# Four direct pairs instead of six in each FFN of an encoder layer, with the row factors, the first granule and the down projection's waits rearranged

## The chip, the cores and the metric

The kernel runs on one core of a Trainium2 chip. The metric is the device time of one execution in microseconds. A core has the matrix engine TensorE (PE), VectorE (DVE), ScalarE (ACT), GpSimd (POOL) and SyncE (SP), which here only issues DMAs. Each engine works through its own instructions in order, and semaphores are all that ties one to another.

## The reference, cut to what matters

One encoder layer on x of 512 rows and 1024 columns in float32:

```python
x = x + 0.5 * swiglu(rms(x, g_ffn1), w_up1, w_down1)      # FFN 1, r = 0
x = x + mixer(rms(x, g_mix))                              # attention, Fourier mix, gates
x = x + 0.5 * swiglu(rms(x, g_ffn2), w_up2, w_down2)      # FFN 2, r = 1
out = rms(x, g_final)

def swiglu(h, w_up, w_down):                              # D_FF = 2816
    gate, up = split(h @ w_up)
    return (silu(gate) * up) @ w_down
```

`rms` divides each row by the root of its mean square (plus 1e-6) and multiplies by a gain. The change touches only the two FFNs and the way x comes in.

## The kernel before, in words

Everything is held transposed: features on the 128 partitions, the 512 rows of x along the free axis. x is 8 tiles of 128 x 512, the activations of an FFN are 22 tiles (`a_t`). Each float32 factor is split into a high part, rounded to the format that TensorE multiplies at its faster rate (`_hi`, by ScalarE, line 575), and the remainder (`_lo`, by VectorE: line 953 for weights, 957 for other tensors, 1121 for the weights of window pairs). A product is then three passes: high by high, high by low, low by high.

A *granule* is 128 columns of a weight matrix with all its input tiles: for the up projection 8 tiles, so 24 matmuls of 512 columns (`granule`; lines 1484 and 1485 are the passes with the high weights, 1496 the pass with the low ones, 1489 that pass where it goes tile by tile). Its weights go through four slots: `raw` (DMA on SP), `w_hi`, `w_lo`. A slot is loaded again when `w_lo_ready` says that the remainder four granules earlier is made, and split again when `w_used` says that TensorE is done with it. A *pair* is one tile of gate and the tile of up that belongs to it.

Each FFN has two ways for a pair. The first six pairs are *direct*: two granules, whose banks VectorE multiplies by the row factors `rstd` (`gate`, `up`); then ScalarE takes silu and VectorE multiplies (`swish`). The row factors are thus not needed when the product starts, only when its bank is read. They come from the squares (ScalarE), added up by GpSimd (line 1430), summed over the partitions by tiny matmuls (`sum_squares`, line 1520), then mean (VectorE, 990), power (GpSimd, 1434), diagonal (VectorE, 978) and a broadcast by a matmul with ones (`spread_factors`, 1527). The other sixteen pairs are *window pairs*: a pair's 1024 x 256 weights and h are cut into 2 x 2 blocks and multiplied by a scheme with seven products of blocks instead of eight (`pair_frame`, lines 1593, 1595, 1599). It needs h with its row factors applied (`normed_h`, 1095), four differences of h blocks (`T_1` to `T_4`, on GpSimd, 1443), the high part and remainder of seven such blocks (`t_rounded`, `t_rest`), and for each pair four sums of weight blocks: two on VectorE (`sums`, 1111 and 1112), two on GpSimd (s2 and s4, 1450 and 1452). A frame's weights are four groups, G0 to G3. In a frame TensorE runs G0 x T_B11, G0 x T_2, the last product of the pair before, G1 x T_B21, G1 x T_4, G2 x T_1 and G2 x T_3; before the last of these it waits for `u2`, a sum that VectorE forms (1128).

All this preparation is interleaved by hand into the direct pairs. There is no planner: the order on each engine is the order of the lines in `direct_pairs` (one function for ScalarE, one for VectorE) and, for GpSimd, the four differences and then two sums per pair. TensorE runs the direct granules (`ffn_up`), the frames, and `ffn_down`. In the down projection a block of 128 output columns is four granules that split the 22 activation tiles by `DOWN_TILES`; the first block waits for the rounding of the activations (`a_rounded`, `a_rest`, in the order `CONV`, two tiles a step), once for each granule.

At the start x comes in four DMA pieces of two tiles, and the weights of granules 0 to 3 behind or between them. TensorE transposes the tiles (`x_tile`, 1536). `X_ORDER` is the order in which ScalarE and VectorE take the transposed tiles: "h" makes the high part and remainder of the unscaled h, "x" copies the tile, "s" squares it, "w" splits a weight granule.

## Time and profile before

| | us |
|---|---|
| median of 3 runs (1012.06 to 1014.20) | 1013.02 |
| the profiled execution | 1014.11 |
| its span, first to last instruction | 1012.3 |

| engine | busy us | share of the span |
|---|---|---|
| PE, matmuls | 997.7 | 99% |
| DVE | 679.0 | 67% |
| ACT | 440.1 | 43% |
| POOL | 198.1 | 20% |

Busy time of PE counts every microsecond in which a matmul is under way; matmuls overlap, so their durations (0.39 us for one of 512 columns) are longer than the distance between their starts (0.23 us). The profiled execution's mean granted TensorE clock is 0.995 of 2.4 GHz. In this profile the first FFN's direct granules run from 12.4 to 83.3 us, its frames to 243.3, the down projection behind it; the second FFN's first up granule starts at about 650 and its first frame at 717.

### The profile page before, as it was taken

The numbers are of one execution on the slowest core, as the hardware profiler recorded it, in microseconds if no ns is written. First come the engines' busy times: TensorE is split into PE (matmuls) and PEld (weight loads), VectorE is DVE, ScalarE is ACT, GpSimd is POOL, SyncE is SP. The second block draws the span as 40 slices with busy tenths as digits, with TensorE's granted clock in tenths as the row PEclk, the third lists the DMA queues.
The fourth block names the chain that finished last, engine by engine and source line by source line (L and its number), as shares of the span: only waits on it lengthen the run. The fifth ranks groups of instructions, "written<-read, shape, count | busy, mean of one in ns | idle before, by whom it ended". The sixth has DMA issues, their size and how long they took to land. (4 is left out here: it accounts for less than half of the span.)

```text
span 1012.3 us, 16276 instructions
## 1 busy us (share of the span) xinstructions
PE 997.7 (99%) x5872; PEld 885.7 (87%) x5872; DVE 679.0 (67%) x924; ACT 440.1 (43%) x656; POOL 198.1 (20%) x113
## 2 busy tenths in 40 slices
PE   8999999999999999999999999999999999999997
PEld 7789999999788888888888888888999999978887
DVE  5778999999534346667765555458899999943332
ACT  5344444446322325346664334334445454633322
POOL 2452333340011110000000001324234333001101
PEclk9999999999999999999999999999999999999999
DMA  6423334323433364212213343322333332333222
GB/s 210 132 66 94 116 92 120 87 83 96 124 96 90 115 171 125 63 42 62 63 42 89 98 124 104 104 84 72 96 108 100 110 97 83 89 117 96 88 68 84
DMA packets 191816, 98.81 MB, mean 98 GB/s; under 512 B 13384, under 2 KB 190616, under 8 KB 191648
## 3 DMA queue, kind: packets, MB, share of 16 engines
q1 hardware_dynamic: 190560, 95.50, 32.3%
q10 hardware_dynamic: 1216, 2.78, 0.8%
q8 instruction: 25, 0.41, 0.2%
q14 instruction: 15, 0.12, 0.0%
HBM read 96.15 MB, written 2.11 MB: 97 GB/s over the span
## 5 line engine op out<-in xcount | busy, mean ns | idle before, releaser
L575 ACT ACTIVATE w_hi<-raw 128x1024 fp32r<-128x1024 f32 (+2 forms) x202 | 181.5, 902 | 231.6 <-PE bank L1496 155.2
L953 DVE TENSOR_TENSOR w_lo<-raw,w_hi 128x1024 fp32r<-128x1024 f32 (+2 forms) x138 | 150.0, 1089 | 145.7 <-ACT w_hi L575 144.2
L1595 PE MATMUL bank<-t_lo,w_hi 128*128 128x256 f32 x896 | 224.7, 283 | 0.0
L1593 PE MATMUL bank<-t_hi,w_hi 128*128 128x256 f32 x896 | 224.6, 283 | 0.0
L1595 PEld LDWEIGHTS bank<-t_lo,w_hi 128*128 128x128 f32 x896 | 172.0, 192 | 0.2
L1593 PEld LDWEIGHTS bank<-t_hi,w_hi 128*128 128x128 f32 x896 | 172.0, 192 | 0.2
L1430 POOL TENSOR_TENSOR ssum<-ssum,sq 128x512 f32<-128x512 f32 x27 | 41.4, 1533 | 535.2 <-ACT sq L612 534.4
L1599 PE MATMUL bank<-t_hi,w_lo 128*128 128x256 f32 x896 | 144.0, 283 | 0.0
L1484 PE MATMUL bank<-a_hi,w_hi 128*128 128x512 f32 (+1 forms) x374 | 140.6, 380 | 1.7 <-ACT a_hi L575 1.7
L1485 PE MATMUL bank<-a_lo,w_hi 128*128 128x512 f32 (+1 forms) x374 | 139.4, 377 | 0.0
L1599 PEld LDWEIGHTS bank<-t_hi,w_lo 128*128 128x128 f32 x896 | 123.6, 192 | 0.0
L1121 DVE TENSOR_TENSOR w_lo<-raw,w_hi 128x1024 fp32r<-128x1024 f32 x64 | 90.9, 1420 | 9.3 <-ACT w_hi L575 9.3
L575 ACT ACTIVATE w_hi<-raw_b 128x1024 fp32r<-128x1024 f32 x64 | 60.8, 949 | 80.0 <-POOL raw_b L1450 40.4
L1121 DVE TENSOR_TENSOR w_lo<-raw_b,w_hi 128x1024 fp32r<-128x1024 f32 x64 | 92.8, 1449 | 3.8 <-ACT w_hi L575 3.7
L1496 PE MATMUL bank<-a_hi,w_lo 128*128 128x512 f32 (+1 forms) x374 | 91.1, 377 | 0.0
L1484 PEld LDWEIGHTS bank<-a_hi,w_hi 128*128 128x128 f32 x374 | 70.3, 188 | 15.4 <-ACT a_hi L575 2.5
L1484 PE MATMUL bank<-h_hi,w_hi 128*128 128x512 f32 x208 | 81.9, 394 | 0.3 <-DVE ga_t L1270 0.3
L1485 PEld LDWEIGHTS bank<-a_lo,w_hi 128*128 128x128 f32 x374 | 70.4, 188 | 12.6
L1485 PE MATMUL bank<-h_lo,w_hi 128*128 128x512 f32 x208 | 81.1, 390 | 0.0
L1496 PEld LDWEIGHTS bank<-a_hi,w_lo 128*128 128x128 f32 x374 | 67.8, 188 | 12.9
L1484 PE MATMUL bank<-hf_hi,w_hi 128*128 128x512 f32 x192 | 76.2, 397 | 0.0
L1485 PE MATMUL bank<-hf_lo,w_hi 128*128 128x512 f32 x192 | 75.7, 394 | 0.0
(230 smaller groups left out, 1494.6 us busy)
## 6 DMA issues: line engine op xcount, KB each, us to landing
raw<-in_w_down_dram SPq DMA_DIRECT2D x48, 384.0 KB, 3.0
raw_b<-in_w_up_dram SPq DMA_DIRECT2D x64, 256.0 KB, 3.7
raw<-in_w_up_dram SPq DMA_DIRECT2D x64, 256.0 KB, 3.6
raw<-in_w_up_dram SPq DMA_DIRECT2D x24, 512.0 KB, 3.9
raw<-in_w_in_dram SPq DMA_DIRECT2D x22, 512.0 KB, 3.7
raw<-in_w_down_dram SPq DMA_DIRECT2D x32, 128.0 KB, 2.2
raw<-in_w_out_dram SPq DMA_DIRECT2D x8, 512.0 KB, 3.4
x_rows<-in_x_dram SPq DMA_DIRECT2D x4, 512.0 KB, 7.8
```

What stands on the lines that cost most here:

```text
L575: return nc.scalar.activation(dst, src, ACT.Copy, scale=scale)
L953: vec.tensor_tensor(w_lo[:, s, 0:nk, :], raw[:, s, 0:nk, :], w_hi[:, s, 0:nk, :].bitcast(F32), ALU.subtract).then_inc(w_lo_ready, 1)
L1121: vec.tensor_tensor(w_lo[:, slot, 0:nk, :], pair_raw[q % 2][:, slot, 0:nk, :], w_hi[:, slot, 0:nk, :].bitcast(F32), ALU.subtract).then_inc ...
L1430: nc.gpsimd.tensor_tensor(ssum[:, :], ssum[:, :], sq[:, m % 2, :], ALU.add).then_inc(sum_added, 1)
L1484: nc.tensor.matmul(out_ap, w_hi[:, s, k, :], xh, start=first and i == 0, stop=False)
L1485: mm = nc.tensor.matmul(out_ap, w_hi[:, s, k, :], xl, start=False, stop=False)
L1496: mm = nc.tensor.matmul(out_ap, w_lo[:, s, k, :], x_parts(k)[0], start=False, stop=last and i == len(tiles) - 1)
L1593: nc.tensor.matmul(out_ap, w_hi[:, slot, at_ + k, :], hi[:, k, :], start=first and k == 0, stop=False, skip_group_check=not first)
L1595: nc.tensor.matmul(out_ap, w_hi[:, slot, at_ + k, :], lo_[:, k, :], start=False, stop=False, skip_group_check=not first)
L1599: mm = nc.tensor.matmul(out_ap, w_lo[:, slot, at_ + k, :], hi[:, k, :], start=False, stop=k == HK - 1, skip_group_check=not first)
```

## The change

Of 22 pairs in each FFN, four are direct and eighteen are window pairs. The row factors' squares are summed inside granule 2 and broadcast ahead of granule 3 in the first FFN, and summed behind granule 0 and broadcast inside granule 1 in the second. Only two tiles of x are transposed ahead of granule 0; four more stand before its tile 2 and the last two before its tile 4, and `X_ORDER` changes with it. In the first block of the down projection TensorE waits for every second tile instead of once for each granule, the tiles of the last granule are taken in the order 0, 1, 20, 21, and ScalarE and VectorE take three more conversions ahead of the last split. The steps of `direct_pairs` are put in a new order on both engines.

```diff
@@ -38,12 +38,12 @@
 SLOTS = 4
 BANKS = 4
 
-DOWN_TILES = [list(range(14, 20)), list(range(2, 8)), list(range(8, 14)), [20, 21, 0, 1]]
+DOWN_TILES = [list(range(14, 20)), list(range(2, 8)), list(range(8, 14)), [0, 1, 20, 21]]
 DOWN_PARTS = [len(tiles) for tiles in DOWN_TILES]
 assert sorted(sum(DOWN_TILES, [])) == list(range(FK)) and len(DOWN_PARTS) == SLOTS
 
 
-DIRECT = 6
+DIRECT = 4
 PAIRS = FK - DIRECT
 assert DIRECT % 2 == 0 and PAIRS % 2 == 0
 UP_GRANULES = 2 * DIRECT + SLOTS * PAIRS
@@ -106,10 +106,9 @@
 
 
 X_BANKS = 6
-X_ORDER = [("h", 0), ("w", 0), ("h", 1), ("h", 2), ("x", 0), ("h", 3), ("h", 4), ("x", 1), ("h", 5),
-           ("h", 6), ("s", 0), ("h", 7), ("x", 2), ("w", 1), ("x", 3), ("x", 4), ("s", 1), ("s", 2),
-           ("s", 3), ("x", 5), ("x", 6), ("x", 7), ("w", 2), ("s", 4), ("s", 5), ("s", 6), ("s", 7),
-           ("w", 3)]
+X_ORDER = [("h", 0), ("w", 0), ("h", 1), ("x", 0), ("x", 1), ("h", 2), ("s", 0), ("h", 3), ("s", 1), ("x", 2),
+           ("h", 4), ("h", 5), ("s", 2), ("x", 3), ("h", 6), ("h", 7), ("x", 4), ("x", 5), ("x", 6), ("x", 7),
+           ("w", 1), ("s", 3), ("s", 4), ("s", 5), ("s", 6), ("s", 7), ("w", 2), ("w", 3)]
 NREL = 2 * WINDOW + 1
 ROWS = 4 * DK + 2 * DK
 
@@ -478,12 +477,14 @@
             def down(r, m, j, n=0):
                 g = G_DOWN[r] + j
                 cols = slice(m * P, (m + 1) * P) if isinstance(m, int) else bass.ds(sp.snap(m * P), P)
-                k0, nk = DOWN_TILES[j][0], DOWN_PARTS[j] if j < SLOTS - 1 else 2
-                load(g, raw[:, g % SLOTS, 0:nk, :], w_down[r][:, k0:k0 + nk, cols], m, n)
-                if j == SLOTS - 1:
-                    k1 = DOWN_TILES[j][2]
+                if j < SLOTS - 1:
+                    k0, nk = DOWN_TILES[j][0], DOWN_PARTS[j]
+                    load(g, raw[:, g % SLOTS, 0:nk, :], w_down[r][:, k0:k0 + nk, cols], m, n)
+                else:
+                    k0, k1 = DOWN_TILES[j][0], DOWN_TILES[j][2]
+                    load(g, raw[:, g % SLOTS, 2:4, :], w_down[r][:, k1:k1 + 2, cols], m, n)
                     cols = slice(m * P, (m + 1) * P) if isinstance(m, int) else bass.ds(sp.snap(m * P), P)
-                    sp.dma_start(raw[:, g % SLOTS, nk:2 * nk, :], w_down[r][:, k1:k1 + nk, cols]).then_inc(down_second, 16)
+                    sp.dma_start(raw[:, g % SLOTS, 0:2, :], w_down[r][:, k0:k0 + 2, cols]).then_inc(down_second, 16)
 
 
             xv = x[0].rearrange("(t p) d -> p t d", p=P)
@@ -651,28 +652,22 @@
                     direct_hi(r, j)
                 silu(r, 0)
                 silu(r, 1)
+                t_rounded(r, T_B11)
                 direct_hi(r, 7)
+                t_rounded(r, T_1)
+                t_rounded(r, T_B21)
+                t_rounded(r, T_2)
                 if r == 0:
                     act.wait_ge(row_ready, 1)
                     act.dma_start(bias_rows, bias_row[:, :]).then_inc(bias_stored, 16)
-                t_rounded(r, T_B11)
-                direct_hi(r, 8)
-                t_rounded(r, T_1)
-                t_rounded(r, T_B21)
-                direct_hi(r, 9)
-                t_rounded(r, T_2)
+                t_rounded(r, T_4)
                 silu(r, 2)
-                t_rounded(r, T_4)
-                direct_hi(r, 10)
                 t_rounded(r, T_3)
                 t_rounded(r, T_B22)
-                silu(r, 3)
-                direct_hi(r, 11)
                 group_hi(r, 0, G0)
-                silu(r, 4)
                 group_hi(r, 0, G1)
                 group_hi(r, 0, G2)
-                silu(r, 5)
+                silu(r, 3)
 
             def t_rounded(r, t):
 
@@ -763,13 +758,12 @@
                 for i in (4, 5, 6):
                     a_rounded(r, CONV[i])
                 split_hi(g + 2)
-                a_rounded(r, CONV[7])
+                for i in (7, 8, 9):
+                    a_rounded(r, CONV[i])
                 silu_c12(r, q)
-                a_rounded(r, CONV[8])
                 act.wait_ge(w_used, g + 1)
                 split_hi(g + 3)
-                for i in (9, 10):
-                    a_rounded(r, CONV[i])
+                a_rounded(r, CONV[10])
 
             def turned_rows(m, odd):
 
@@ -1042,51 +1036,44 @@
                 nrm = NORM_FFN1 if r == 0 else NORM_FFN2
                 direct_lo(r, 4)
                 mean(nrm)
-                direct_lo(r, 5)
                 diagonal(nrm)
-                direct_lo(r, 6)
+                if r == 0:
+                    direct_lo(r, 5)
                 factors(nrm)
                 gate(r, 0)
                 up(r, 0)
+                for i in range(HK):
+                    normed_h(nrm, i)
+                if r == 1:
+                    direct_lo(r, 5)
                 gate(r, 1)
+                swish(r, 0)
+                for i in range(HK, DK):
+                    normed_h(nrm, i)
+                direct_lo(r, 6)
                 up(r, 1)
-                swish(r, 0)
                 if r == 0:
                     constants()
-                for i in range(HK):
-                    normed_h(nrm, i)
                 swish(r, 1)
+                t_rest(r, T_B11)
                 direct_lo(r, 7)
-                for i in range(HK, DK):
-                    normed_h(nrm, i)
-                direct_lo(r, 8)
+                t_rest(r, T_2)
                 gate(r, 2)
+                t_rest(r, T_B21)
+                sums(r, 0)
                 up(r, 2)
+                t_rest(r, T_4)
                 swish(r, 2)
-                t_rest(r, T_B11)
-                t_rest(r, T_2)
-                direct_lo(r, 9)
+                t_rest(r, T_1)
+                group_lo(r, 0, G0)
                 gate(r, 3)
-                t_rest(r, T_B21)
-                up(r, 3)
-                direct_lo(r, 10)
-                swish(r, 3)
-                t_rest(r, T_4)
-                t_rest(r, T_1)
-                direct_lo(r, 11)
-                sums(r, 0)
-                gate(r, 4)
                 t_rest(r, T_3)
-                group_lo(r, 0, G0)
-                up(r, 4)
-                swish(r, 4)
+                group_lo(r, 0, G1)
                 t_rest(r, T_B22)
-                group_lo(r, 0, G1)
-                gate(r, 5)
                 group_lo(r, 0, G2)
                 sums(r, 1)
-                up(r, 5)
-                swish(r, 5)
+                up(r, 3)
+                swish(r, 3)
 
             def normed_h(n, m):
 
@@ -1192,12 +1179,12 @@
                 for i in (4, 5, 6):
                     a_rest(r, i)
                 split_lo(g + 2)
+                a_rest(r, 7)
+                a_rest(r, 8)
                 c12(r, q)
-                a_rest(r, 7)
+                a_rest(r, 9)
                 swiglu(r, q)
-                a_rest(r, 8)
                 split_lo(g + 3)
-                a_rest(r, 9)
                 a_rest(r, 10)
 
             def residual(n, m, o, scale, it=0, per=0):
@@ -1467,8 +1454,7 @@
                 return mm
 
             def granule(g, out_ap, x_parts, first=True, last=True, it=0, n=0, tiles=None, x_ready_at=None, done=True,
-                        by_tile=False,
-                        between=None):
+                        by_tile=False, between=None, inside=None):
 
 
 
@@ -1478,6 +1464,8 @@
                 for i, k in enumerate(tiles):
                     if between and by_tile:
                         between(k)
+                    if inside and k == DK // 2:
+                        inside()
                     if x_ready_at:
                         x_ready_at(k)
                     xh, xl = x_parts(k)
@@ -1547,7 +1535,7 @@
             pe.wait_ge(ident_ready, 2)
             pe.wait_ge(gain_landed, 16)
             nc.tensor.transpose(banks[0][:, 0:DK], gain_rows[:, :], ident[0:DK, 0:DK]).then_inc(gain_turned, 1)
-            for m in range(X_BANKS):
+            for m in range(2):
                 x_tile(m)
 
             def other_constants():
@@ -1561,8 +1549,8 @@
 
             def x_rest(k):
 
-                if k in (2, 4):
-                    x_tile(X_BANKS + k // 2 - 1)
+                for m in {2: range(2, 6), 4: range(6, DK)}.get(k, ()):
+                    x_tile(m)
 
             def ffn_up(r, it, first=False, n=SLOTS):
                 nrm = NORM_FFN1 if r == 0 else NORM_FFN2
@@ -1572,14 +1560,17 @@
                         pe.wait_ge(out_read, o - 3 + n * it)
                     if first and r == 0 and j >= 2:
                         pe.wait_ge(x_ready, DK)
+                    if first and r == 0 and j == 3:
+                        spread_factors(nrm)
                     granule(g, banks[o % BANKS][:, :], hf_parts, it=it, n=n, by_tile=first and j == 0,
                             x_ready_at=h_ready(nrm) if first and j == 0 else None,
                             between=x_rest if first and r == j == 0 else
-                            (lambda: spread_factors(nrm)) if first and j == 3 else None)
-                    if first and j == 2:
+                            (lambda: spread_factors(nrm)) if first and r == 1 and j == 1 else None,
+                            inside=(lambda: sum_squares(nrm)) if first and r == 0 and j == 2 else None)
+                    if first and r == 1 and j == 0:
                         sum_squares(nrm)
-                        if r == 0:
-                            other_constants()
+                    if first and r == 0 and j == 2:
+                        other_constants()
 
             def product(r, q, it, group, at_, t, out_ap, first=True):
 
@@ -1651,14 +1642,18 @@
                     for j in range(SLOTS):
                         g = G_DOWN[r] + SLOTS * c + j
 
-                        if first and c == 0:
-                            if j == 1:
-                                last_product(r, PAIRS - 1)
-                            need = len(CONV) * r + 1 + max(CONV.index(i // 2) for i in DOWN_TILES[j])
-                            pe.wait_ge(a_hi_ready, need)
-                            pe.wait_ge(a_lo_ready, need)
+                        if first and c == 0 and j == 1:
+                            last_product(r, PAIRS - 1)
+
+                        def a_ready(k, tiles=DOWN_TILES[j]):
+
+                            if k % 2 == 0:
+                                need = len(CONV) * r + 1 + CONV.index(tiles[k] // 2)
+                                pe.wait_ge(a_hi_ready, need)
+                                pe.wait_ge(a_lo_ready, need)
+
                         granule(g, banks[o % BANKS][:, :], a_parts(DOWN_TILES[j]), first=j == 0, last=j == SLOTS - 1,
-                                it=it, n=n)
+                                it=it, n=n, x_ready_at=a_ready if first and c == 0 else None)
                         if r == 1 and j == 1 and not (first and c == 0):
                             turn_rows(2 * it + c - 1, 1 - c)
```

## Rows read from the trace of the kernel before

**Rows 1.** The page, part 1: busy time, share of the span, instructions

```profile
PE 997.7 (99%) x5872; PEld 885.7 (87%) x5872; DVE 679.0 (67%) x924; ACT 440.1 (43%) x656; POOL 198.1 (20%) x113
```

**Rows 2.** Waits of TensorE, longest first: us in total, times, longest

```profile
PE bank L1536 <- DMA x_rows<-in_x_dram: 3.2, 1, 3.2
...
PE bank L1484 <- ACT a_hi L575: 1.7, 2, 0.9
```

**Rows 3.** TensorE's timeline, start to 75 us: start, duration, engine, line, operation

```profile
9.29 3.35 PE L1536 MATMUL bank<-ident,x_rows 128*128 128x128 f32 x16 [3.19 <-DMA x_rows<-in_x_dram]
...
30.16 1.05 PE L1520 MATMUL bank<-ones,ssum 128*128 128x2 f32 x8 [0.25 <-POOL ssum L1430]
...
31.86 0.50 PE L1484 MATMUL bank<-hf_hi,w_hi 128*128 128x512 f32 x1
...
37.22 1.02 PE L1527 MATMUL bank<-gb_t,ones 128*128 128x512 f32 x2
...
39.92 0.41 PE L1484 MATMUL bank<-hf_hi,w_hi 128*128 128x512 f32 x1
...
65.37 1.98 PE L1496 MATMUL bank<-hf_hi,w_lo 128*128 128x512 f32 x8
...
70.81 1.98 PE L1496 MATMUL bank<-hf_hi,w_lo 128*128 128x512 f32 x8
```

**Rows 4.** The same view in the pair frames

```profile
88.77 0.64 PE L1599 MATMUL bank<-t_hi,w_lo 128*128 128x256 f32 x4
...
90.21 0.64 PE L1599 MATMUL bank<-t_hi,w_lo 128*128 128x256 f32 x4
```

**Rows 5.** Busy time in one stretch, with TensorE's granted clock

```profile
33.00:34.00 1.00, 1.00 (x4) 0.72 (x3) 0.53 (x1) 0.00 (x0) 1.00 (x1) 0.50 1.03 304
```

**Rows 6.** VectorE's timeline before the first pair frame

```profile
38.28 0.69 DVE L984 COPY rstd<-bank 128x512 f32<-128x512 f32 x1 [1.82 <-PE bank L1527]
...
46.83 2.72 DVE L1095 SCALAR_TENSOR_TENSOR t_sum<-xT,consts,rstd 128x512 f32<-128x512 f32 x4
...
49.48 1.20 DVE L953 TENSOR_TENSOR w_lo<-raw,w_hi 128x1024 fp32r<-128x1024 f32 x1
...
58.51 4.56 DVE L957 TENSOR_TENSOR t_lo<-t_sum,t_hi 128x1024 fp32r<-128x1024 f32 x2
...
71.60 0.68 DVE L1111 TENSOR_TENSOR raw_b<-raw_b 128x512 f32<-128x512 f32 x1
...
72.81 0.68 DVE L1015 TENSOR_TENSOR ga_t<-bank,rstd 128x512 f32<-128x512 f32 x1
...
73.41 1.71 DVE L957 TENSOR_TENSOR t_lo<-t_sum,t_hi 128x1024 fp32r<-128x1024 f32 x1
...
75.17 2.19 DVE L1121 TENSOR_TENSOR w_lo<-raw_b,w_hi 128x1024 fp32r<-128x1024 f32 x1
...
86.64 0.42 DVE L1128 TENSOR_TENSOR u_t<-bank,p_t 128x256 f32<-128x256 f32 x1 [1.04 <-PE bank L1599]
```

**Rows 7.** GpSimd's differences and additions by line: least, median, longest ns

```profile
L1443 POOL TENSOR_TENSOR t_sum<-t_sum x8: 2401/2866/7701, 45.2 to 690.7; 128x1024 f32<-128x1024 f32 x8
...
L1430 POOL TENSOR_TENSOR ssum<-ssum,sq x27: 1289/1457/2092, 18.6 to 989.6; 128x512 f32<-128x512 f32 x27
```

**Rows 8.** Timelines at 28 and at 656 us, three engines

```profile
27.86 3.88 ACT L575 ACTIVATE w_hi<-raw 128x1024 fp32r<-128x1024 f32 x4
...
656.63 1.23 DVE L953 TENSOR_TENSOR w_lo<-raw,w_hi 128x1024 fp32r<-128x1024 f32 x1 [2.93 <-ACT w_hi L575]
...
658.91 1.98 PE L1496 MATMUL bank<-hf_hi,w_lo 128*128 128x512 f32 x8
...
667.15 0.16 DVE L990 TENSOR_SCALAR var<-bank 128x4 f32<-128x4 f32 x1 [9.29 <-PE bank L1520]
...
667.50 1.28 ACT L646 ACT_TABLE_LOAD   x1
...
669.35 0.87 DVE L978 TENSOR_SCALAR gb_t<-ident,rinv 128x128 f32<-128x128 f32 x4 [0.91 <-POOL rinv L1434]
```

## The prediction, made before the changed kernel was run

> **What bounds the kernel now.** I read the page's busy times first: TensorE is busy 99% of the span, so only its own instructions and its rare waits can set the time [rows 1]. The list of waits shows how rare they are: 3.2 us for x's arrival, and 1.7 us in two equal waits for ScalarE's rounding of the activations, one at the head of each down projection [rows 2]. Then TensorE's timeline, for the price of what is exchanged. A direct granule repeats every 5.44 us (65.37 and 70.81), so a direct pair costs 10.88; a product of the seven-product scheme repeats every 1.44 us (88.77 and 90.21), so a pair costs 7 x 1.44 = 10.08 [rows 3, 4]. Last I read VectorE's and GpSimd's timelines between the row factors and the first pair frame, because the change takes 21.8 us of TensorE time away from that stretch. There the reader is to see that VectorE hardly rests, and that its operations on two SBUF tensors and GpSimd's shut each other out [rows 6, 7].
>
> Sums are made against the profiled execution: 1014.11 us for a span of 1012.3. The median of the runs shown is 1013.02, 1.09 below; I apply the difference to the median. About 0.2% (2.0 us) is what a measurement can tell from nothing.
>
> **Four pairs moved from direct to seven products.** 4 x (10.88 - 10.08) = -3.2 us, certain as TensorE work at full clock.
>
> **Down projection waits by tile.** The third granule of the first column block waited for all six tiles though the first four were ready. With waits by tile, and with tiles 10 to 13 rounded before the last pair's swish, the two waits go: -1.7 us [rows 2]. What is late next is tiles 20, 21; they need VectorE's last product, split and remainder, but [0, 1, 20, 21] puts them 0.9 us into a granule that starts after the removed wait. I estimate they arrive level with it. Ends: -1.7 and, if the last product is late by as much, 0.
>
> **The start.** Tiles 0 and 1 of granule 0 now run before x's second piece lands at 9.29, in time in which TensorE waited [rows 2, 3]. But VectorE's low halves come at 9.3, so tile 1 runs behind the landing, and ScalarE and VectorE now alternate squares and copies with the h tiles; I follow both and get granule 0 done within 0.2 us of before. Then a new wait: the third granule's split stands behind the eighth square on ScalarE, and that square waits for GpSimd's fifth addition. The additions need at least 1.29 us each, 1.46 in the median [rows 7], the third can't start before about 18.8 (behind the split of granule 1), so the square ends at 24.4 and the split, 0.97 us apiece [rows 8], at 25.4; granule 1 ends at 24.2. TensorE waits 1.2 us. Against it, the factors are now taken earlier: squares summed inside granule 2 (1.0), constants (0.7) and then the broadcast. It needs split, sum, power and diagonal on VectorE and GpSimd: VectorE reaches the mean at about 29.9 behind three w_lo, and from the mean's start to the diagonal's end is 3.07 us (667.15 to 670.22) [rows 8]. So the broadcast starts at about 33.0, 0.4 after TensorE is free. It keeps TensorE 0.9 (37.22 to 39.92 is 2.70 with 1.81 of low products behind it) [rows 3], granule 3 takes 5.44, and granule 4 starts at 39.3 instead of 39.92: -0.6 us. This includes 1.7 us gained because the clock need not fall: at 33 to 34 us the granted clock was 0.50, which is 1.2 of 2.4 GHz, after a wait and 1.7 us of tiny matmuls (30.16 to 31.86), and from 31.86 to 39.92 stand 8.06 us for 0.89 + 5.44 = 6.33 of work: 1.7 lost [rows 3, 5]. If it falls here too, the term is +1.1; if it also stays full at 9 us, -1.6.
>
> **Row factors in the second FFN.** Sums behind granule 0, broadcast inside granule 1. Granule 1's high products end at 658.91 + 0.95 = 659.86. VectorE takes the mean only behind w_lo of granule 4, which ends at 657.86; plus 3.07, the diagonal is there at 660.95. TensorE had 0.5 us to spare here and now waits +1.1 us, with the low products queued behind it [rows 8]. Ends: 0.9 and 1.3.
>
> **The first pair frame of the first FFN.** This decides. Count from the broadcast's start E. Before, the frame began at E + 46.2 (37.22 to 83.4: 2.70 and eight granules). Now it begins at E + 0.89 + 5 x 5.44 = E + 28.1. Its last product needs VectorE's u2, 7.2 us later: E + 35.3. Before, that need was E + 53.4, and VectorE began u2 at 86.64 = E + 49.4 [rows 6]. VectorE's work from the factors' copy (E + 1.06) to u2, free of interference, by pitch: 0.60 for a 512-wide product (71.60 to 72.81 for two), 0.66 for a scaled h (46.83 to 49.48 for four), 1.14 for a remainder of 1024 (1.20 with the end overlapping) [rows 6]. Now it is: factors' copy, gate 0 and up 0, 1.9; eight scaled h, 5.3; the other two gates and up 1 to 3 with the third gate, 3.6 for six; four swish, 2.4; w_lo 6 and 7, 2.3; seven t remainders, 8.0; two pairs of sums, 2.4; three group remainders, 3.4; constants 0.5. Together 29.8: ready at E + 30.9, 4.4 us before the need.
>
> But GpSimd must place four 1024-wide differences and three 512-wide ones in it. How they interfere is in the rows: the remainder at 73.41 took 1.71 instead of 1.20, the one at 75.17 took 2.19, two at 58.51 took 4.56 instead of 2.35; each time it is GpSimd's rest, and one t difference took 7.7 us where the median is 2.87 and the least 2.40 [rows 6, 7]. So I take them as exclusive: 2.4 us for a wide difference, 1.2 for a narrow one (72.81 to 73.98). That is 4 x 2.4 + 3 x 1.2 = 13.2 us, less what falls beside VectorE's operations that read a bank (gates, ups, constants: at most 4.1). Before, 5.7 us of idle VectorE took two of them for nothing; that idle time is gone. Bounds: u2 at E + 30.9 (no exclusion: no loss) and E + 30.9 + 13.2 = E + 44.1 (+8.8). Placed in program order, I get: four scaled h until 5.6; T_1's difference beside gate 1 and into swish 0, until 8.2; scaled h 4 to 7 and w_lo 6 until 12.5; T_2 beside up 1 until 15.0; swish 1, T_4, B11, w_lo 7 and T_3 in either order, and T_2's remainder at E + 23.8 whichever side gets the turns, since all of it excludes itself; then gate 2, B21, sums, up 2 until 27.4, the narrow difference s2 until 28.0, and s4 among T_4, swish 2, T_1 and G0. So G0's remainder ends at E + 32.0 to 33.2 (needed at E + 29.1), and after gate 3, T_3, G1, B22, G2, sums, up 3, the next s2 and swish 3, u2 at E + 41.2 to 41.8: +6.0 us, about 3 to 4 of it at G0 and the rest before T_3. Waiting behind w_lo and u2 on TensorE is the whole frame, and behind that all that follows. Frames 1 to 17 then run as before, VectorE having slack in each.
>
> The Trainium skill ("SBUF — State Buffer", section "Who interferes with whom") says that a VectorE instruction with two SBUF inputs and a GpSimd instruction that reads SBUF block each other fully, and one with a single SBUF input does not. The trace agrees: 2.19 at 75.17 against 0.68 for a gate. By the rule the term is the 6.0 above; were it only a slowdown in proportion, it would be half.
>
> **The same frame in the second FFN.** Here the broadcast is two granules earlier, so the need is at E + 42.5. But gate 1 waits for granule 2, and silu 0 stands behind the split of granule 6 and a table load of 1.28 us, which was hidden at 667.50 [rows 8]. So swish 0 comes at E + 11.2, the chain runs 3.0 us behind that of the first FFN, and u2 comes at E + 44.2 to 44.8: +2.0 us (ends: 0 and 3).
>
> **Clock after the new waits.** Two waits of 2 to 4 us within 10 us; a fall costs the 1.7 above where TensorE is the bound, but between the two waits it isn't. I take +0.8 (0 to 3.4). "TensorE: Matmul & The Clock Gate" in the Trainium skill (section "HAM oscillation — how this bites in real kernels") warns that waits between bursts of matmuls bring the clock down each time; the half clock at 33 us after sparse work agrees, and by it this term would be 1.7 to 3.4.
>
> No other queue is in the way: SP issues the window loads after seven or eight w_lo as before and they land before the sums need them; POOL's order is unchanged; only the bias row's store moves on ScalarE's queue.
>
> **Sum.** -3.2 - 1.7 - 0.6 + 1.1 + 6.0 + 2.0 + 0.8 = +4.4: 1013.0 + 4.4 = 1017.4 us.
>
> **Rivals.**
> A. The preparation stays hidden: GpSimd's work falls in bank-reading operations and costs VectorE nothing, so terms of 6.0, 2.0 and 0.8 go: 1013.0 - 4.4 = 1008.6, faster. For it: before, VectorE was ahead by 4.0 us at u2 and idle for 6.7. Against it: 4.4 us of slack must hold 9.1 or more of exclusive work. It decides from the point where the blocked time is under 4.4.
> B. Half late: the first frame waits 4.0, the second FFN's doesn't, the clock stays: -4.4 + 4.0 = -0.4, 1012.6. For it: 9.1 - 4.4 = 4.7 is the least the budget allows, and the last narrow difference can fall behind u2 (-1.2).
> C. As forecast, and the clock falls at each wait and at the start: 1017.4 + 1.7 + 1.7 = 1020.8.
>
> Chances: forecast 0.52 (own range 1014.8 to 1019.5), A 0.16, B 0.20, C 0.12. The range 1010.5 to 1020.5 leaves out most of A and the upper half of C. Slower by over 0.2%: forecast and C, 0.64; within: B without its lower edge, 0.19; faster 0.17.
>
> **What the profile after would show.** TensorE waiting for VectorE's w_lo or u2 at about 61 to 75 us, 6 us in all, and VectorE without idle time from 34 on; t differences with GpSimd durations far over 2.4; a wait of 1.2 us for the split before the third granule; 1.1 us for the diagonal in the second FFN; no wait at the activations' rounding; granted clock 1.00 near 33 us; first activation product of the down projection at about 247 to 248 instead of 243.3. I am wrong if TensorE runs through the first frame: then VectorE's remainders aren't held up as I have placed them, and the time is A's.

## The result, and the profile after

The changed kernel takes 1016.15 us (median of 7 executions, 1015.56 to 1017.14) where the kernel before takes 1013.02 (median of 7): the ratio is 1.0035, with a 95% interval of 1.0024 to 1.0045. It is slower by 3.1 us. The profiled execution took 1016.41 us for a span of 1014.6, which is 2.3 above that of before. Lines below are those of the changed kernel.

Part 1 of the page, against [rows 1]:

```profile
PE 998.2 (98%) x6016; PEld 891.4 (88%) x6016; DVE 704.8 (69%) x948; ACT 448.1 (44%) x672; POOL 207.8 (20%) x121
```

TensorE's list of waits, against [rows 2]:

```profile
PE bank L1590 <- DVE w_lo L1108: 2.7, 1, 2.7
PE bank L1584 <- DVE u_t L1115: 2.0, 2, 1.5
...
PE bank L1472 <- ACT w_hi L576: 1.9, 2, 1.1
```

Busy time is 0.5 us more and not 3.2 less: time at half clock and short waits count as busy in it, so it is not where a change of this size is read. The two waits for a_hi are gone; in their place stand waits for VectorE's w_lo and u2, and for ScalarE's split. Where they fall is in TensorE's timeline of the first FFN (start, duration, engine, line, operation, idle time before it and its releaser):

```profile
11.23 3.59 PE L1524 MATMUL bank<-ident,x_rows 128*128 128x128 f32 x16
...
26.27 0.47 PE L1472 MATMUL bank<-hf_hi,w_hi 128*128 128x512 f32 x1 [0.79 <-ACT w_hi L576]
...
33.57 1.13 PE L1515 MATMUL bank<-gb_t,ones 128*128 128x512 f32 x2
...
62.09 0.39 PE L1584 MATMUL bank<-t_hi,w_hi 128*128 128x256 f32 x1 [0.16 <-ACT w_hi L576]
...
66.06 1.22 PE L1590 MATMUL bank<-t_hi,w_lo 128*128 128x256 f32 x4 [2.75 <-DVE w_lo L1108]
...
74.44 0.39 PE L1584 MATMUL bank<-t_hi,w_hi 128*128 128x256 f32 x1 [0.47 <-DVE u_t L1115]
...
75.98 0.28 PE L1584 MATMUL bank<-t_hi,w_hi 128*128 128x256 f32 x1
```

x's transposes start 1.9 us later than before (11.23 against 9.29 in [rows 3]); the third granule waits 0.79 for its split; the broadcast is at 33.57, so E = 33.57. The first frame starts at 62.09, stops for 2.75 us after its first eight matmuls and again at its last product, and the next frame follows at 75.98. In the kernel before the same two frames began like this:

```profile
83.50 0.28 PE L1593 MATMUL bank<-t_hi,w_hi 128*128 128x256 f32 x1
...
92.13 0.28 PE L1593 MATMUL bank<-t_hi,w_hi 128*128 128x256 f32 x1
```

(The prediction read 83.4 for the first.)

VectorE's timeline of the same stretch, against [rows 6]:

```profile
34.73 0.69 DVE L978 COPY rstd<-bank 128x512 f32<-128x512 f32 x1 [0.84 <-PE bank L1515]
...
39.91 2.53 DVE L1022 TENSOR_TENSOR a_t<-ga_t,ua_t 128x512 f32<-128x512 f32 x1
...
48.95 3.42 DVE L951 TENSOR_TENSOR t_lo<-t_sum,t_hi 128x1024 fp32r<-128x1024 f32 x1
...
52.30 3.41 DVE L947 TENSOR_TENSOR w_lo<-raw,w_hi 128x1024 fp32r<-128x1024 f32 x1
...
64.79 1.21 DVE L1108 TENSOR_TENSOR w_lo<-raw_b,w_hi 128x1024 fp32r<-128x1024 f32 x1
...
73.98 0.41 DVE L1115 TENSOR_TENSOR u_t<-bank,p_t 128x256 f32<-128x256 f32 x1
```

Behind 34.73 no row has an idle time before it until 74.6. A swish product at 39.91 took 2.53 us instead of 0.68, a remainder at 48.95 took 3.42 instead of 1.20. GpSimd's timeline shows what ran beside them: the first t difference at 39.48, and the other three in one piece, 3.15 us each. The last fence has the eight of the two FFNs by line, against [rows 7]:

```profile
39.48 2.42 POOL L1430 TENSOR_TENSOR t_sum<-t_sum 128x1024 f32<-128x1024 f32 x1 [7.62 <-DVE t_sum L1082]
45.17 9.46 POOL L1430 TENSOR_TENSOR t_sum<-t_sum 128x1024 f32<-128x1024 f32 x3 [3.28 <-DVE t_sum L1082]
```

```profile
L1430 POOL TENSOR_TENSOR t_sum<-t_sum x8: 2416/3314/3377, 39.5 to 684.1; 128x1024 f32<-128x1024 f32 x8
```

A table of the stages, each number but the span the start of an instruction in the two timelines of TensorE:

| us | before | after | moved by |
|---|---|---|---|
| granule 4, first FFN | 39.92 | 40.02 | +0.1 |
| first frame | 83.50 | 62.09 | -21.4 (21.76 of direct work less) |
| second frame | 92.13 | 75.98 | -16.2 |
| first down projection | 243.33 | 247.71 | +4.4 |
| attention block, first h_hi matmul | 365.9 | 368.9 | +3.0 |
| second FFN | 649.84 | 652.81 | +3.0 |
| second down projection | 876.83 | 880.51 | +3.7 |
| span | 1012.3 | 1014.6 | +2.3 |

Each FFN's up part loses time (4.4 and 0.7 us) and each down projection gives back 1.4.

### The profile page after: what moved, and what is told of

The parts are those of the page before. It is cut to its first block, busy times and chain, and to the rows that moved or that the text cites. A ratio compares the mean times of both kernels' runs of the same rounds, so it can differ in the third digit from the quotient of the medians.

```text
span 1014.6 us, 16714 instructions
## 1 busy us (share of the span) xinstructions
PE 998.2 (98%) x6016; PEld 891.4 (88%) x6016; DVE 704.8 (69%) x948; ACT 448.1 (44%) x672; POOL 207.8 (20%) x121
## 4 chain that ended last, share of the span: by engine, by line
PE 89%; DVE 5%; ACT 2%; issue 2%; POOL 1%; DMA 1%; POOLq 0%; ACTq 0%; SPq 0%; DVEq 0%
PE bank L1472 17%; PE bank L1473 17%; PE bank L1484 16%; PE bank L1584 11%; PE bank L1590 11%; PE bank L1586 11%; DVE w_lo L1108 1%; ACT w_hi L576 1%; DVE t_lo L951 1%; PE bank L1477 1%; PE bank L1756 1%; PE bank L1449 1%; PE bank L1448 1%; PE bank L1453 1%; DMA raw<-in_w_up_dram 1%
## 5 line engine op out<-in xcount | busy, mean ns | idle before, releaser
L1584 PE MATMUL bank<-t_hi,w_hi 128*128 128x256 f32 x1008 | 253.9, 284 | 2.4 <-DVE u_t L1115 2.0
L1586 PE MATMUL bank<-t_lo,w_hi 128*128 128x256 f32 x1008 | 253.4, 284 | 0.0
L1584 PEld LDWEIGHTS bank<-t_hi,w_hi 128*128 128x128 f32 x1008 | 194.0, 192 | 3.7 <-DVE u_t L1115 2.4
L1586 PEld LDWEIGHTS bank<-t_lo,w_hi 128*128 128x128 f32 x1008 | 194.0, 192 | 0.1
L1590 PE MATMUL bank<-t_hi,w_lo 128*128 128x256 f32 x1008 | 162.8, 284 | 2.7 <-DVE w_lo L1108 2.7
L1590 PEld LDWEIGHTS bank<-t_hi,w_lo 128*128 128x128 f32 x1008 | 139.8, 193 | 3.0 <-DVE w_lo L1108 3.0
L1108 DVE TENSOR_TENSOR w_lo<-raw,w_hi 128x1024 fp32r<-128x1024 f32 x72 | 103.4, 1437 | 6.2 <-ACT w_hi L576 6.2
L1108 DVE TENSOR_TENSOR w_lo<-raw_b,w_hi 128x1024 fp32r<-128x1024 f32 x72 | 102.5, 1424 | 3.7 <-ACT w_hi L576 3.7
L1472 PE MATMUL bank<-hf_hi,w_hi 128*128 128x512 f32 x128 | 51.7, 404 | 1.9 <-ACT w_hi L576 1.9
L1437 POOL TENSOR_TENSOR raw<-raw 128x512 f32<-128x512 f32 x18 | 30.1, 1672 | 114.0 <-DVE raw L1098 114.0
```

What stands on the lines that cost most here:

```text
L1108: vec.tensor_tensor(w_lo[:, slot, 0:nk, :], pair_raw[q % 2][:, slot, 0:nk, :], w_hi[:, slot, 0:nk, :].bitcast(F32), ALU.subtract).then_inc ...
L1437: nc.gpsimd.tensor_tensor(s2, a22, s3, ALU.subtract).then_inc(s2_ready, 1)
L1472: nc.tensor.matmul(out_ap, w_hi[:, s, k, :], xh, start=first and i == 0, stop=False)
L1584: nc.tensor.matmul(out_ap, w_hi[:, slot, at_ + k, :], hi[:, k, :], start=first and k == 0, stop=False, skip_group_check=not first)
L1586: nc.tensor.matmul(out_ap, w_hi[:, slot, at_ + k, :], lo_[:, k, :], start=False, stop=False, skip_group_check=not first)
L1590: mm = nc.tensor.matmul(out_ap, w_lo[:, slot, at_ + k, :], hi[:, k, :], start=False, stop=k == HK - 1, skip_group_check=not first)
```

## Experiments

Each was timed beside the kernel before on the same chip; its ratio is to that. The theory: VectorE and GpSimd exclude each other in the preparation, which makes u2 of the first pair late, and all else is small.

**1, 2. The tile waits alone**, in the kernel before (t1_tiles), with the rounding order of the last pair that belongs to them. The same kernel was run again as e11_tiles; it is called kernel 1 below.

```
-DOWN_TILES = [..., [20, 21, 0, 1]]
+DOWN_TILES = [..., [0, 1, 20, 21]]
...
-                            pe.wait_ge(a_hi_ready, need)
+                        def a_ready(k, tiles=DOWN_TILES[j]):
+                            if k % 2 == 0:
+                                need = len(CONV) * r + 1 + CONV.index(tiles[k] // 2)
...
```

> The kernel before with one part of the change alone: waits by tile in the first block of the down projection, its tiles in the order 0, 1, 20, 21, and the conversions ahead of the last split. If the term is what the two removed waits were (0.86 and 0.88 us), it is 1.7 us faster than before: 1011.3. If what the two traces show between the first and the last granule of that block holds (1.4 us in each FFN), 2.8 us faster: 1010.2. If the last product of VectorE takes the wait's place: 1013.

> The kernel before with waits by tile once more, beside e9 on the same chip, to compare the two: 1009.7 us as in its first runs. The theory has it ahead of e9 by 1.5 to 3 us, since six direct pairs hide what four don't.

1009.73 us, ratio 0.9972 (0.9962 to 0.9982), and 1010.73, ratio 0.9981 (0.9972 to 0.9989): -3.4 and -2.0 us. From the first activation product to the first of the attention block it takes 121.1 us (241.5 to 362.6) where the kernel before takes 122.6. Worth 1.4 us in each FFN, not 0.85. Why more than the wait: before, 13.74 us pass from the first product to the third granule's low pass (243.33 to 257.07), after it 12.4 (247.7 to 260.1); 0.86 of the difference is the wait in brackets; the other 0.5 has no bracket.

**3. The t differences at half width.** Half of each difference is left out of the computation, filled with zeros; VectorE's work stays whole.

```
+                        nc.gpsimd.memset(t_sum[:, to, HK // 2:HK, :], 0.0)
-                        nc.gpsimd.tensor_tensor(t_sum[:, to, :, :], ...
+                        nc.gpsimd.tensor_tensor(t_sum[:, to, 0:HK // 2, :], ...
```

> The changed kernel with GpSimd's four t differences only half as wide (the other half is filled with zeros, so half of each difference is left out of the computation). VectorE's work and all waits are unchanged. Theory (GpSimd's and VectorE's operations on two SBUF tensors exclude each other, and that makes VectorE late): each difference holds the port 1.2 us less, VectorE reaches the last u2 some 4 us earlier, TensorE's waits for VectorE in the first frames (2.7, 0.5 and 1.5 us) all but go, and with them the half clock: 1010 to 1012 us. Rival (VectorE's own work is too much for four direct pairs, whatever GpSimd does): the waits stay, 1015 to 1016.

1009.53 us, ratio 0.9966 (0.9956 to 0.9976): 6.6 us faster than the change. TensorE's waits, and u2 on VectorE's timeline:

```profile
PE bank L1473 <- ACT w_hi L576: 1.7, 2, 1.0
...
PE bank L1585 <- DVE u_t L1115: 1.2, 1, 1.2
```

```profile
69.62 0.41 DVE L1115 TENSOR_TENSOR u_t<-bank,p_t 128x256 f32<-128x256 f32 x1
```

The wait for w_lo is gone, u2 comes 4.4 us earlier, with VectorE's own instructions unchanged. Only GpSimd's time was taken away, so it was GpSimd's time that made VectorE late.

**4. The change with the old start of the first FFN** (x's order, squares and broadcast as before):

```
-X_ORDER = [("h", 0), ("w", 0), ("h", 1), ("x", 0), ("x", 1), ("h", 2), ("s", 0), ...
+X_ORDER = [("h", 0), ("w", 0), ("h", 1), ("h", 2), ("x", 0), ("h", 3), ("h", 4), ...
-                    if first and r == 0 and j == 3:
-                        spread_factors(nrm)
```

> The changed kernel with the start of the kernel before in the first FFN: six tiles of x transposed first, the old X_ORDER, squares summed behind granule 2 and the broadcast inside granule 3. Granule 4 then starts at about 39.9 us as in both kernels, but the broadcast at about 37.2 instead of 33.6. Theory (the first frame is set by VectorE, whose chain starts with the broadcast): all behind the first frame comes 3.6 us later, 1019 to 1020 us, and TensorE's waits in the first frame grow by as much. Rival (TensorE sets the time and the earlier broadcast is worth only what it saves of TensorE's own time): 1016 to 1016.5.

1018.08 us, ratio 1.0051 (1.0036 to 1.0067), 1.9 us slower than the change, between the two expectations. In its timeline of TensorE:

```profile
36.49 1.02 PE L1516 MATMUL bank<-gb_t,ones 128*128 128x512 f32 x2
...
39.19 0.39 PE L1473 MATMUL bank<-hf_hi,w_hi 128*128 128x512 f32 x1
...
64.85 0.38 PE L1583 MATMUL bank<-t_hi,w_hi 128*128 128x256 f32 x1 [3.72 <-ACT w_hi L577]
...
78.74 0.28 PE L1583 MATMUL bank<-t_hi,w_hi 128*128 128x256 f32 x1
```

Granule 4 begins at 39.19, 0.8 earlier than in the change; the second frame begins at 78.74, 2.76 later, and E is 2.92 later. So the new start is worth nothing on TensorE. It is worth E, because VectorE's chain counts from there. Part of the 2.92 is the clock and not the order: in this execution it fell at the start, as it did before the change:

```profile
33.00:34.00 1.00, 1.00 (x4) 0.82 (x3) 1.00 (x5) 0.00 (x0) 0.00 (x0) 0.50 1.15 347
```

Where it stayed up, in the two executions of kernel 1 (experiment 9), the same start has E at 35.39 and 34.73 instead of 36.49.

**5. The power beside a remainder.** In the changed kernel the diagonal went ahead of w_lo 5; this puts it back.

```
                 mean(nrm)
-                diagonal(nrm)
                 if r == 0:
                     direct_lo(r, 5)
+                diagonal(nrm)
```

> The changed kernel with VectorE's split of granule 5 moved between the mean and the diagonal in the first FFN, where the kernel before had it. Theory (VectorE's split and GpSimd's power exclude each other): the power takes 1.9 us instead of 1.02, the diagonal and the broadcast come 0.9 us later, and since the first frame is set from there, 1017.0 us. Rival (the power takes 1.02 because of something else): the split ends before the power does, nothing moves, 1016.2 us.

1016.19 us, ratio 1.0035 (1.0023 to 1.0047): no difference that the runs can tell. GpSimd's power and TensorE's broadcast in the timeline:

```profile
30.14 1.94 POOL L1421 TENSOR_TENSOR rinv<-var,half 128x4 f32<-128x4 f32 x1 [3.50 <-DVE var L984]
...
33.13 1.10 PE L1515 MATMUL bank<-gb_t,ones 128*128 128x512 f32 x2 [0.18 <-DVE gb_t L972]
```

and in the changed kernel the same power in the two FFNs:

```profile
30.83 1.02 POOL L1421 TENSOR_TENSOR rinv<-var,half 128x4 f32<-128x4 f32 x1 [3.50 <-DVE var L984]
...
660.98 1.02 POOL L1421 TENSOR_TENSOR rinv<-var,half 128x4 f32<-128x4 f32 x1 [3.17 <-DVE var L984]
```

Beside a remainder the power takes 1.94, without it 1.02. In the first FFN that moves next to nothing: TensorE waits 0.18 us for the diagonal here, and in the change it gets to the broadcast after the diagonal anyhow (33.57, the diagonal ends at 32.76).

**6, 7, 8. VectorE's order by need.** e6_order puts G0, T_3 and u2 ahead of work that is needed later; e7_w2 also splits granule 2's weights ahead of the last two squares; e9_tail mends what e6_order made late, with c2 of the first pair ahead of G3 and up 3 last, and on ScalarE G1's high part ahead of a silu.

```
# e6_order
                 t_rest(r, T_4)
+                group_lo(r, 0, G0)
                 swish(r, 2)
+                gate(r, 3)
+                group_lo(r, 0, G1)
                 t_rest(r, T_1)
-                group_lo(r, 0, G0)
...
+                t_rest(r, T_3)
+                u2(r, 0)
+                t_rest(r, T_B22)
+                group_lo(r, 1, G0)
                 up(r, 3)
# e7_w2, besides
-           ("w", 1), ("s", 3), ("s", 4), ("s", 5), ("s", 6), ("s", 7), ("w", 2), ("w", 3)]
+           ("w", 1), ("s", 3), ("s", 4), ("s", 5), ("w", 2), ("s", 6), ("s", 7), ("w", 3)]
# e9_tail, in the products of the first pair, over e6_order
+                if not q:
+                    c2(r, 0)
+                    group_lo(r, 0, G3)
+                    group_lo(r, 1, G1)
+                    up(r, 3)
+                    swish(r, 3)
```

> The changed kernel with VectorE's steps ahead of the first frame in the order in which TensorE needs them: G0's remainder ahead of swish 2 and T_1, G1's ahead of T_1, u2 and G0 of the next pair ahead of up 3 and swish 3. Nothing is added or taken away. Theory (the waits come from VectorE's order and from too little time, some 2 us too little in the first FFN, none in the second): TensorE's 2.7 us wait at G0 falls under 1, frame 1 of the first FFN starts at about 73 us instead of 76.0, the second FFN's 1.5 us wait goes: 1011.6 us. Rival (the sum of VectorE's work decides, and an order only moves the wait to another product): 1015 to 1016 us.

> The reordered kernel with ScalarE's and VectorE's split of granule 2 ahead of the last two squares at the start, instead of behind them. Theory (the third granule waits only for that split, 0.8 us in the changed kernel, and the broadcast is set by TensorE's own work from there): everything behind comes 0.8 us earlier, 1010.8 us. Rival (the last squares come 1 us later and the sum of squares, inside granule 2, takes over the wait): no difference to the reordered kernel, 1011.6 us.

> The reordered kernel (e6), which traded TensorE's wait at G0 for one of 3.0 us at the last product of pair 0 (behind c2(0) on VectorE, which stood behind up 3, swish 3 and G1's split, that on ScalarE behind a silu that waits for swish 3). Now c2(0) stands ahead of G3, up 3 and swish 3 behind G1 of the next pair, and G1's high part ahead of that silu. Same work. Theory (four direct pairs leave VectorE some 2 us too little in the first FFN and enough in the second, if each step stands where its product needs it): waits of 2 to 3 us in the first FFN, under 1 in the second, 1011 to 1013 us. Rival (the order moves the wait once more): 1015 us or more.

All three are misses, and slower: 1019.76 (ratio 1.0075, 1.0062 to 1.0089), 1024.29 (1.0122, 1.0106 to 1.0137), 1020.71 (1.0077, 1.0064 to 1.0090). TensorE's waits of e6_order and the row behind the longest of them:

```profile
PE bank L1586 <- DVE ua_t L1126: 5.9, 2, 3.0
PE bank L1592 <- DVE w_lo L1110: 2.4, 3, 1.0
```

```profile
80.42 0.39 PE L1586 MATMUL bank<-t_hi,w_hi 128*128 128x256 f32 x1 [2.96 <-DVE ua_t L1126]
```

and TensorE's longest wait of e9_tail:

```profile
PE bank L1590 <- ACT p_t L576: 4.4, 2, 2.2
```

In e6_order the second frame did begin at 72.7, as I had worked out. But what had been put back was needed 8 us on: 2.96 us for ua_t at 80.4, the same in the second FFN, and the down projection at 250.5 instead of 247.7. VectorE has no slack from 34.7 to 74.6, so each of the three orders only chose who waits, and chose worse; that no order would do better is not shown. In e7_w2 another wait took the place of the split's: 1.7 us for GpSimd's last sum. Its trace is of the fastest of its four executions (1020.98); why the others took up to 4 us more is open.

**9. The squares inside granule 3**, in kernel 1, to see whether earlier factors pay there.

```
+                            inside=(lambda: sum_squares(nrm)) if first and r == 0 and j == 3 else None)
```

> The kernel before with waits by tile (six direct pairs), and in the first FFN the squares summed inside granule 3 instead of behind granule 2, the split of granule 5 behind the diagonal. The tiny matmuls no longer stand in one piece with the wait and the constants. Theory (they brought the clock down to half at 32.6 us, 1.7 us lost): granted clock 1.00 at 33 us, 1.7 us off the 1009.7 of the kernel with waits by tile: 1008.0 us. Rival (the clock falls anyway, or the first gate is late for granule 4 and takes the time back): 1009 to 1010 us.

1010.49 us, ratio 0.9981 (0.9972 to 0.9990): level with kernel 1. TensorE waits 0.71 us for ga_t at 38.85. In kernel 1 there was nothing to get in the two executions that have a profile. The clock rows of 33 to 34 us (last three columns: granted clock, DMA share, GB/s), first of t1_tiles, then of e11_tiles:

```profile
33.00:34.00 1.00, 1.00 (x6) 0.82 (x5) 0.29 (x1) 0.00 (x0) 1.00 (x1) 1.00 1.12 328
```

```profile
33.00:34.00 1.00, 1.00 (x6) 0.84 (x5) 0.44 (x3) 0.00 (x0) 0.53 (x1) 1.00 0.96 281
```

Both are 1.00 where [rows 5] and the execution of experiment 4 have 0.50, with the same instructions on TensorE.

**10. The change without its tile waits.**

```
+                        if first and c == 0:
...
+                            need = len(CONV) * r + 1 + max(CONV.index(i // 2) for i in DOWN_TILES[j])
+                            pe.wait_ge(a_hi_ready, need)
```

> The changed kernel without its tile waits in the down projection (order and waits there as before). If the parts add up, it is slower than the changed kernel by what the tile waits alone gave, 3.4 us: 1019.5 us. If they were worth only the 1.7 us of the two waits: 1017.8 us.

1019.24 us, ratio 1.0062 (1.0048 to 1.0077), 3.1 us slower than the change, and the 1.7 us of waits for a_hi are back. The parts add up: 2.0 to 3.4 us in kernel 1, 3.1 here.

**11, 12. The t differences on VectorE**, the whole computation kept; e13_sums moves the first pair's s2 and s4 too.

```
                 gate(r, 1)
+                difference(r, 0)
...
+            def difference(r, i):
...
+                vec.tensor_tensor(t_sum[:, to, :, :], t_sum[:, one, :, :], t_sum[:, two, :, :],
+                                  ALU.subtract).then_inc(t_formed, 1)
...
-                        nc.gpsimd.tensor_tensor(t_sum[:, to, :, :], ...
# e13_sums, besides
+                    vec.tensor_tensor(s2, a22, s3, ALU.subtract).then_inc(s2_ready, 1)
```

> The changed kernel with the four t differences moved from GpSimd to VectorE, each right behind what it reads; the computation is whole. VectorE gets 4 x 1.14 = 4.6 us more work per FFN. Theory (the two engines exclude each other, so a difference costs VectorE 2.4 us when GpSimd makes it and 1.14 when it makes it itself): 4 x 1.26 = 5.0 us less in the chain, less what of GpSimd's fell beside bank reads; VectorE reaches the last u2 about 3 to 4 us earlier than in the changed kernel (74.0 and 706.8), G0's remainder is in time or under 1 us late, the half clock goes: 1010 to 1011.5 us. Rival (more work on the engine that is late makes it later): 1018 us or more.

> The same, and the two narrow differences s2 and s4 of pair 0 on VectorE too (0.6 us each instead of 1.2 of exclusion and the hand-over to GpSimd). Theory: another 1 us off the chain, G0's remainder in time in both FFNs, 1009 to 1010.5 us, level with or just ahead of the kernel before with waits by tile (1009.7 and 1010.7 in two sets of runs). Rival: they fell beside bank reads and cost nothing on GpSimd, so no difference to the one without, or 1 us slower.

1010.99 us, ratio 0.9986 (0.9977 to 0.9995), and 1011.69, ratio 0.9985 (0.9976 to 0.9994). So VectorE is given 4 x 1.2 us more work and the kernel is 5.2 us faster than the change. The timelines of VectorE and TensorE in e12_diffs:

```profile
39.50 1.22 DVE L1088 TENSOR_TENSOR t_sum<-t_sum 128x1024 f32<-128x1024 f32 x1
40.63 0.69 DVE L1022 TENSOR_TENSOR a_t<-ga_t,ua_t 128x512 f32<-128x512 f32 x1
...
50.06 1.20 DVE L951 TENSOR_TENSOR t_lo<-t_sum,t_hi 128x1024 fp32r<-128x1024 f32 x1
51.19 1.21 DVE L947 TENSOR_TENSOR w_lo<-raw,w_hi 128x1024 fp32r<-128x1024 f32 x1
...
70.63 0.41 DVE L1128 TENSOR_TENSOR u_t<-bank,p_t 128x256 f32<-128x256 f32 x1
...
71.09 0.39 PE L1590 MATMUL bank<-t_hi,w_hi 128*128 128x256 f32 x1 [1.87 <-DVE u_t L1128]
```

The swish product that took 2.53 takes 0.69, the remainders that took 3.42 and 3.41 take 1.20 and 1.21. u2 is at 70.63 instead of 73.98, and one wait of 1.87 is left there; the second FFN's wait of 1.50 is gone. The sums on VectorE gain nothing more: the two ratios are the same.

**The fastest version** is kernel 1 (1009.73 and 1010.73), with e12_diffs level (1010.99). Both beat both kernels. e12_diffs holds the tile waits as well, so the four pairs taken from direct work, -3.2 us by themselves, earn about nothing even there: 2.1 us of waits stay in its first frame (0.27 and 1.87), and on TensorE the start is no gain (below).

## Why the prediction was right, point by point

The direction, the mechanism and its place were right; the time was 1.3 us high (1017.4 against 1016.15). The sum over the profiled spans was +4.4 and came out +2.3:

| term | forecast | measured |
|---|---|---|
| four pairs | -3.2 | -3.2 (at the pitches of before) |
| start, until the first frame | -0.6 | +0.35 |
| first frame, first FFN, with its clock | +6.8 | +5.25 |
| tile waits, two FFNs | -1.7 | -2.8 |
| factors and first frame, second FFN | +3.1 | +2.3 |
| frames behind the first, rest | 0 | +0.4 |

How they are read: the first frame starts 21.4 us earlier (83.50 to 62.09) for 21.76 of work less, so the start is +0.35. From first to second frame it takes 13.89 us instead of 8.63 (83.50 to 92.13): +5.25. The second FFN's up part is 0.7 longer for 1.6 of work less. The 0.4 stands in the second frame of each FFN, without a bracket (78.38 to 80.19 and 711.19 to 712.99 are 1.8 us each where a product takes 1.44); e12_diffs has it too, and its cause is open.

**The first frame: right, and its budget nearly exact.** I had VectorE's free work from E to u2 end at E + 30.9, and 9.1 of GpSimd's time excluded: E + 40.0, and E + 41.2 to 41.8 when placed in order. Measured: u2 starts at 73.98 = E + 40.4. The excess of VectorE's rows over their free durations, from 34.7 to 74.4, is 1.85 + 1.2 + 2.2 + 2.2 + 0.5 + 1.1 + 0.4 = 9.4. G0's remainder ended at E + 32.4 (forecast E + 32.0 to 33.2) and its wait was 2.75 (3 to 4). Placement in order cost less than I had it, by 0.8 to 1.4. In e12_diffs E is 33.16, the free work ends at E + 30.9 + 4 x 1.2 = E + 35.7, s2 and s4 still hold VectorE up by 2.0 (1.71, 1.78 and 1.04 in place of 1.20, 0.68 and 0.68), and u2 starts at E + 37.5, 2.2 behind the need at E + 35.3.

**The clock behind the wait: mis-sized.** It fell, as [rows 5] had it fall:

```profile
66.00:69.50 3.50, 3.44 (x17) 3.44 (x18) 3.50 (x5) 1.01 (x2) 0.00 (x0) 0.53 0.00 0
69.50:74.00 4.50, 4.47 (x38) 4.26 (x36) 4.46 (x7) 0.46 (x1) 2.10 (x2) 1.00 0.77 219
```

(the same view; clock 0.53 and 1.00). Of the 5.25 us, the half clock is 1.5: 16 matmuls took 3.43 us (66.06 to 69.49) where 16 x 0.12 = 1.92 is the full pace. The two stops inside the frame are 2.75 + 0.47 = 3.2 in brackets, and the rest is stopping and starting. But TensorE would have waited for u2 in that time: the last product began at 74.44, behind u2, where 62.09 + 7.2 = 69.3 was the need, and that is the whole 5.1. The +0.8 should have been nothing. In the second FFN there is one wait of 1.50 and the clock stays at 1.00. The Trainium skill ("TensorE: Matmul & The Clock Gate", section "HAM oscillation — how this bites in real kernels") warns that waits between bursts bring the clock down each time. Of the two waits of over 1 us in the first frames it fell at one, and it is not always the longer wait that brings it down: in e10_no_tiles the clock stayed at 1.00 behind the 2.75 us for w_lo and fell to 0.50 behind the 1.88 us for u2.

**The tile waits: mis-sized**, -2.8 instead of -1.7. An idle time in brackets is not all that a wait costs; 0.5 us of each 1.4 has no bracket.

**The start: this step failed.** I had granule 0 done within 0.2 us of before. Tiles 0 and 1 run ahead of x's second piece, but they wait for VectorE's low halves (w_lo until 9.0, the second hf_lo until 9.7), and the transposes are queued behind them: 11.23 instead of 9.29. Granule 0 gives way to granule 1 at 19.76 instead of 18.87, 0.9 later and not within 0.2; that accounts for the 0.7 that granule 4 is behind the forecast (40.02 for 39.3). Granule 1's last matmul ends at 25.48, the split of granule 2 is 0.8 late all the same, and the broadcast is 0.6 later than forecast, set by TensorE and not by the diagonal. The other half, 1.7 us because the clock need not fall at 33 us, was priced from one execution. With the old start it fell in two profiled executions (before and t3_start: E at 37.22 and 36.49, granule 4 at 39.92 and 39.19) and not in two others (kernel 1: E at 35.39 and 34.73, granule 4 at 38.10 and 37.45). With the new start it fell in none of the eight that have it unchanged (E between 32.85 and 33.57, granule 4 at 40.02 in the change and 39.5 in t4_lo5). So the new start brings E 1.2 to 4.4 us forward and gives TensorE itself nothing: granule 4 comes up to 2.6 us later than with the old start at full clock. Some of the spread is when x's second piece lands: 9.29, 8.29, 8.64 and 8.12 in the four with the old start; counted from it, E of the old start is 27.9 and 28.2 with the fall and 26.8 and 26.6 without. Whether the new order keeps the clock up is suggested by these counts and not shown. That the fall is not in every execution also fits the two ways of measuring: the profiled execution of before, with the fall, was 1.09 above its median, and the difference of medians (3.1) is 0.8 above that of the spans. No run tells the two apart for certain.

**The factors in the second FFN: this step failed too, by 1.0 us.** The wait for the diagonal, forecast 1.1, was 0.1. TensorE ended the high pass near 662.8 and the broadcast began at 662.96; the power took 1.02 us (experiment 5). The 3.07 us that I carried over from [rows 8] held a power beside w_lo 5, 1.93 long in the trace before, which in the changed order has nothing beside it. It is the same exclusion that I used for the frame, and missed here. The first frame's wait there was right:

```profile
706.79 0.41 DVE L1115 TENSOR_TENSOR u_t<-bank,p_t 128x256 f32<-128x256 f32 x1
...
707.26 0.39 PE L1584 MATMUL bank<-t_hi,w_hi 128*128 128x256 f32 x1 [1.50 <-DVE u_t L1115]
```

u2 at E + 43.8 (forecast 44.2 to 44.8), wait 1.50 (2.0).

Of the rivals, A and B are out: TensorE waited at both frames, and 1008.6 and 1012.6 are far from 1016.15. C is out at the start and in the second FFN; at the first frame the clock did fall. That 1016.15 lies so near 1017.4 is in part luck: the first frame, the clock and the second FFN came out 2.4 us cheaper than forecast and the tile waits gave 1.1 us more, against 1.4 us from the start and the second frames.

## What to carry to other kernels

Before work is taken off the bounding engine ahead of a stage, count the helper engines' chain for that stage from its first input to its last need, and add to it the other engine's time wherever the two exclude each other; the free durations alone would have said 4.4 us of slack here. Each t difference on the "idle" GpSimd kept VectorE up by 1.9 us (1.85 + 1.2 + 2.2 + 2.2 for the four), where VectorE makes it itself in 1.14 at its pitch; the move back brought u2 from E + 40.4 to E + 37.5, which is 4 x 0.7. It was the repair, and three other orders of the same work were not. Waits by tile, on the other hand, gave 2.8 us.

## What the runs showed of the hardware

- A power of 128 x 4 on GpSimd took 1.02 us alone and 1.94 beside a VectorE remainder of 128 x 1024: even a tiny operation is held up by a large one.
- Which engine is blocked varies. In the first FFN before, one t difference took 7.7 us while VectorE ran at its free durations [rows 7]; after, the longest took 3.38 and VectorE's rows carried the loss. In this chain the sum over both engines is what could be forecast.
- The granted clock at 33 us was 0.50 in two executions and 1.00 in two others of the same instructions on TensorE there. Behind the same wait of 1.9 us for u2 it stayed at 1.00 in e12_diffs and fell to about half in e13_sums. A clock seen in one profile is not yet a property of the kernel.
- Sixteen matmuls of x's transposes took 3.1 us at half clock (9.29 to 12.39) and 3.3 at full clock (11.23 to 14.50), and 2.5 in t4_lo5, at half clock until about 12 us, where four later ones took 0.35 (13.86 to 14.21, before). So TensorE waited among them for something that the records show as busy time; for what was not tried.
